# State-space decays from one single-pass product per head over all tokens, and outputs scaled as their roots arrive

## The chip, the cores and the metric

The kernel runs on one core of a Trainium2 chip. The metric is the device time of one execution in microseconds (us), the median of several runs. PE is the matrix engine (TensorE), PEld its weight loads, DVE is VectorE, ACT is ScalarE, POOL is GpSimd, SP is SyncE, which issues the weight DMAs.

## The reference

Two transformer blocks run over 256 tokens of width 1024. The change is in the first mixer of the second block, a state space layer of 16 heads of 64 values in two groups, whose result is independent of how the tokens are cut into chunks:

```
cs = cumsum(a)                       # a = dt * A, one number per token and head
L[l, s] = exp(cs[l] - cs[s]) for l >= s, else 0
y = (C B^T * L) @ X + D_skip * x_heads     # X = x_heads * dt; C, B shared by the 8 heads of a group
y = rmsnorm(y * silu(z)) per group of 512
```

The kernel takes chunks of 128 tokens, so there are two chunks (t = 0, 1), and the second also gets what the first leaves as state.

## The kernel before

The weights come through SP in tiles of 128x1024. Every product with them is made in three single-pass matmuls (fp32r type): ACT rounds a tile to its high part (line 954), DVE subtracts to get the low part (line 1405, `rest_of_tile`), and PE multiplies high by high, high by low and low by high (lines 357 to 359 for outputs with features on the partitions, 387 to 389 with tokens on the partitions). There are five slots for parts, so tile i can be rounded once PE has released tile i-5, and four slots for raw tiles. Small products are made in full fp32 with `group` (line 340); the profile shows one such matmul as two instructions.

All queues are written out by hand in program order. On PE, `step(n)` takes n pieces of the projections that lie ready as a filler (`fill`: z, gq, gk, gv, r, sig2, in this order): one piece of gq, gk or sig2 is 24 matmuls of 256 columns, one piece of z, gv or r is 12 of 512 columns. Four pieces make the two halves of gq: pieces 1 and 2 release the first two tiles, pieces 3 and 4 the next two. On ACT and DVE, `until(v)` first does all tile work, and all evacuations that were put behind (`put_behind`), whose release on PE comes before point v in PE's order; `full(name)` is `until` of that group and then a wait for it. `out_of(name)` waits until a PSUM bank was read, `settle` until the engine's own earlier results have landed.

The state space layer in the kernel before, in order on PE: 16 transposes of the convolved x (`xs`), the small product `dec`, one filler piece (gq 2), the C B^T products `CB` of both groups, and then the decays. There are eight (t, q) with four heads each (q = 0 to 3). For each, DVE multiplies the mask `after` by `a` (`seg_in`, 128x512), PE multiplies this in full fp32 with `upper` (`seg`: four matmuls of 128 columns), which gives cs[l] - cs[s] on the lower triangle, ACT takes Exp out of PSUM (line 1275), DVE multiplies by masked CB into `E`, and PE multiplies E by X (`diag`: four matmuls of 64 columns). After every second diag DVE adds it to the skip product and multiplies by silu(z), ACT sums squares (line 1294), POOL takes the root, DVE scales, and PE transposes (`y_out`) for the later product, with `y_T` on DVE and a rounding on ACT (line 1280). After the last `y_out` come one filler piece, the products `la` of the gated linear attention, and eight filler pieces, while DVE and ACT work out its gates.

Of the kernel before, what the change touches and what calls it, by code (L numbers as in the profile page):

```python
# [9 lines left out]
F32 = mybir.dt.float32  # L10
# [5 lines left out]
P = 128  # L16
# [32 lines left out]
    "pad", "conv_in", "conv", "silu", "gated", "Aexp", "dt", "soft_e", "soft", "soft_exp", "a", "X", "Xd", "La", "E",  # L49
# [34 lines left out]
def chunks(v, n):  # L84
    return v.rearrange("p (c n) -> p c n", c=n)
# [14 lines left out]
def build(nc, a, out):  # L100
    with ExitStack() as ctx:
# [32 lines left out]
        def f32(at, n):  # L134
            return room[:, at:at + n]
# [87 lines left out]
        dt_, e_, s_, s2_, p_, aa = (small[:, 32 * i:32 * i + 32] for i in range(6))  # L223
        Aexp, e1, d0 = (small[:, 192 + 16 * i:208 + 16 * i] for i in range(3))
        dt3 = dt_.rearrange("p (t h) -> p t h", t=2)
        a3 = aa.rearrange("p (t h) -> p t h", t=2)
# [15 lines left out]
        rot = [chunks(f32(8192 + 512 * i, 512), 4) for i in range(6)]  # L242
        La, E = rot[0:3], rot[3:6]
        quads = [(t, q) for t in range(2) for q in range(4)]
# [38 lines left out]
        def tensor(e):  # L283
# [481 lines left out]
            group(psum[:, b, 0:16], [(upper, a3[:, 1, :])])  # L765
            ends(group(psum[:, b, 16:32], [(after, a3[:, 0, :])]), "dec", b)
# [14 lines left out]
            yb = None  # L781

            def diag(i):
                nonlocal yb
                t, q = quads[i]
                g = q // 2
                if q % 2 == 0:
                    yb = bank()
                need(s["E"], i + 1)
                need(s["X"], t + 1)  # L790
                for h in range(4):
                    o = 256 * (q % 2) + 64 * h
                    last = group(psum[:, yb, o:o + 64], [(E[i % 3][:, h, :], X[:, t, 256 * q + 64 * h:256 * q + 64 * h + 64])])
                if q % 2 == 0:
                    where["diag", i] = Group(None, done(last), None)
                    return
                ends(last, ("y", t, g), yb)
                where["diag", i] = where["y", t, g]
                if t:
                    b = bank()  # L800
                    need(s["Xd"], 1)
                    out_of(("CB", g))
                    ends(group(psum[:, b, :], [(CB[:, g, P:256], Xd[:, 512 * g:512 * g + 512])]), ("yx", g), b)

            def y_out(t, g):
                need(s["y_out"], 2 * t + g + 1)
# [130 lines left out]
        def scalar(e):  # L937
# [332 lines left out]
            def seg(i):  # L1270
                full(("seg", i))
                if i >= 3:
                    until(where["diag", i - 3].at)
                    e.wait_ge(s["pe"], where["diag", i - 3].at)
                emptied(e.activation(E[i % 3], chunks(psum[:, where["seg", i].bank, :], 4), ACT.Exp), ("seg", i))

            def y_out(t, g):
                full(("yT", t, g))
                e.wait_ge(s["yT_gain"], 2 * t + g + 1)
# [4 lines left out]
            seg(1)  # L1284
            for i in range(8):
                if i + 2 < 8:
                    seg(i + 2)
                t, g = i // 4, (i % 4) // 2
                if i % 2:
                    full(("y", t, g))  # L1290
                    if t:
                        full(("yx", g))
                    e.wait_ge(s["y_sum"], 2 * t + g + 1)
                    e.activation(junk[:, 512 * g:512 * g + 512], xs[:, t, 512 * g:512 * g + 512], ACT.Square,
                                 accum_out=yss[:, 2 * t + g:2 * t + g + 1]).then_inc(s["y_sq"], 1)
                if i in (2, 4, 6):
                    y_out(*((0, 0), (0, 1), (1, 0))[i // 2 - 1])
            y_out(1, 1)
# [91 lines left out]
        def vector(e):  # L1390
# [387 lines left out]
            conv(3)  # L1778
            until(where["cv", 3].at + 3)
# [26 lines left out]
            e.wait_ge(s["a"], 1)  # L1806

# [6 lines left out]
            def seg_in(i):  # L1814
                t, q = quads[i]
                if i >= 3:
                    until(where["seg", i - 3].at)
                    e.wait_ge(s["pe"], where["seg", i - 3].at)
# [3 lines left out]
            seg_in(0)  # L1822
            seg_in(1)
# [18 lines left out]
            seg_in(2)  # L1842

            def seg(i):
                t, q = quads[i]
                until(where["seg", i].at)
                out_of(("seg", i))
                tt(E[i % 3], E[i % 3], bc(CB[:, q // 2, 256 * t:256 * t + P], 1, [P, 4, P]), ALU.mult).then_inc(s["E"], 1)

            def diag(i):  # L1850
                t, g = i // 4, (i % 4) // 2
                if i % 2 == 0:
                    return
                c, j = slice(512 * g, 512 * g + 512), 2 * t + g
                y = xs[:, t, c]
                step(tt(by_head(y), by_head(y), bc(row("ssd_D_2")[:, 8 * g:8 * g + 8], 2, [P, 8, 64]), ALU.mult))
# [17 lines left out]
                e.wait_ge(s["y_rstd"], j + 1)  # L1874
                ts(y, y, yrs[:, j:j + 1], ALU.mult).then_inc(s["y_out"], 1)

            def y_T(t, g):
                name, n = ("yT", t, g), 2 * t + g + 1
# [10 lines left out]
            seg(1)  # L1889
            for i in range(8):  # L1890
                if i + 3 < 8:
                    seg_in(i + 3)
                if i + 2 < 8:
                    seg(i + 2)
                diag(i)
                if i in (2, 4, 6):
                    y_T(*((0, 0), (0, 1), (1, 0))[i // 2 - 1])
            y_T(1, 1)
# [335 lines left out]
```

## Time and profile before

| | |
|---|---|
| median of 3 runs | 983.16 us (983.12 to 984.9) |
| profiled execution, its own time | 984.08 us |
| its span, first to last instruction | 982.0 us |
| PE busy | 963.7 us, 98% |
| DVE busy | 631.8 us, 64% |
| ACT busy | 506.0 us, 52% |
| granted TensorE clock, mean | 0.999 |

The span is what the rows below are times in; 2.1 us of the execution lie around it. Matmuls overlap in the pipeline, so that the rate of PE is read from the distance between starts and not from the duration of one.

### The profile page before, as it was taken

What the parts mean: (1) busy time and instruction counts of PE and PEld (TensorE: products, weight loads), DVE (VectorE), ACT (ScalarE), POOL (GpSimd) and SP (SyncE); (2) the same over time, 40 slices, a digit from 0 to 9 for tenths busy, and PEclk for the clock granted to TensorE, in tenths of its full rate; (3) what the DMA queues carried; (4) which work ended last, traced back from release to release, by engine and by line L of the source; (5) the groups of instructions that cost most, each with busy time, mean ns of one, the idle gap of its engine ahead of it and who ended that gap; (6) DMA issues with size and microseconds to landing.
All of it is one profiled execution on the core that took longest, in us unless ns stands there. A gap on an engine that the chain in (4) does not pass through costs nothing.

```text
span 982.0 us, 15896 instructions
## 1 busy us (share of the span) xinstructions
PE 963.7 (98%) x6552; PEld 871.7 (89%) x6552; DVE 631.8 (64%) x822; ACT 506.0 (52%) x744; POOL 52.5 (5%) x88
## 2 busy tenths in 40 slices
PE   7999999999999999999999999999999999999996
PEld 5877889989998898998988899998998899999995
DVE  5757676677555555687867687775554466555554
ACT  5565645655444444556644575544455444444442
POOL 3000001002000000300000002100100020000000
PEclk9999999999999999999999999999999999999999
DMA  8974445555665656465554556554755446565651
GB/s 272 314 243 129 113 125 154 170 172 173 210 196 175 191 183 198 121 191 171 183 159 114 148 152 193 154 191 129 237 168 155 127 151 211 176 198 175 198 179 43
DMA packets 135079, 170.36 MB, mean 173 GB/s; under 512 B 7664, under 2 KB 99104, under 8 KB 135008
## 3 DMA queue, kind: packets, MB, share of 16 engines
q1 hardware_dynamic: 133472, 165.47, 54.5%
q10 hardware_dynamic: 992, 2.58, 0.8%
q0 software_dynamic: 544, 1.31, 0.5%
q8 instruction: 52, 0.85, 0.4%
q14 instruction: 19, 0.16, 0.1%
HBM read 168.28 MB, written 1.05 MB: 172 GB/s over the span
## 4 chain that ended last, share of the span: by engine, by line
PE 90%; DVE 5%; ACT 3%; issue 1%; DMA 1%; DVEq 0%; POOLq 0%; POOL 0%; SPq 0%; ACTq 0%
PE ps L357 14%; PE ps L358 13%; PE ps L359 13%; PE ps L387 7%; PE ps L389 7%; PE ps L388 7%; PE ps L695 5%; PE ps L694 5%; PE ps L696 5%; PE ps L340 5%; PE ps L436 3%; DVE parts L1405 2%; PE ps L467 1%; PE ps L469 1%; PE ps L468 1%
## 5 line engine op out<-in xcount | busy, mean ns | idle before, releaser
L1405 DVE TENSOR_TENSOR parts<-raws,parts 128x1024 fp32r<-128x1024 f32 (+1 forms) x308 | 367.7, 1211 | 231.2 <-ACT parts L954 230.4
L954 ACT ACTIVATE parts<-raws 128x1024 fp32r<-128x1024 f32 (+1 forms) x308 | 315.6, 1043 | 247.0 <-PE ps L359 135.5
L357 PE MATMUL ps<-room_r,parts 128*128 128x256 f32 x1248 | 352.4, 282 | 0.9 <-DVE parts L1405 0.9
L358 PE MATMUL ps<-room_r,parts 128*128 128x256 f32 x1248 | 348.6, 279 | 0.0
L359 PE MATMUL ps<-room_r,parts 128*128 128x256 f32 x1248 | 348.5, 279 | 0.0
L357 PEld LDWEIGHTS ps<-room_r,parts 128*128 128x128 f32 x1248 | 234.7, 188 | 7.1 <-issue 3.9
L358 PEld LDWEIGHTS ps<-room_r,parts 128*128 128x128 f32 x1248 | 234.6, 188 | 1.3
L359 PEld LDWEIGHTS ps<-room_r,parts 128*128 128x128 f32 x1248 | 234.6, 188 | 0.0
L387 PE MATMUL ps<-parts,room_r 128*128 128x512 f32 (+1 forms) x336 | 136.2, 405 | 2.6 <-DVE parts L1405 2.6
L389 PE MATMUL ps<-parts,room_r 128*128 128x512 f32 (+1 forms) x336 | 132.0, 393 | 0.0
L388 PE MATMUL ps<-parts,room_r 128*128 128x512 f32 (+1 forms) x336 | 131.9, 393 | 0.0
L694 PE MATMUL ps<-parts,room_r 128*128 128x512 f32 x216 | 85.5, 396 | 0.0
L696 PE MATMUL ps<-parts,room_r 128*128 128x512 f32 x216 | 85.4, 396 | 0.0
L695 PE MATMUL ps<-parts,room_r 128*128 128x512 f32 x216 | 85.4, 396 | 0.0
L387 PEld LDWEIGHTS ps<-parts,room_r 128*128 128x128 f32 x336 | 63.9, 190 | 17.7 <-DVE parts L1405 3.2
L389 PEld LDWEIGHTS ps<-parts,room_r 128*128 128x128 f32 x336 | 63.7, 190 | 14.7
L388 PEld LDWEIGHTS ps<-parts,room_r 128*128 128x128 f32 x336 | 64.0, 190 | 13.4 <-issue 0.5
L1439 DVE TENSOR_TENSOR room_r<-room,room_r 128x512 fp32r<-128x512 f32 x43 | 29.8, 693 | 32.5 <-ACT room_r L1209 11.9
L696 PEld LDWEIGHTS ps<-parts,room_r 128*128 128x128 f32 x216 | 40.6, 188 | 9.7
L694 PEld LDWEIGHTS ps<-parts,room_r 128*128 128x128 f32 x216 | 40.6, 188 | 8.8
L695 PEld LDWEIGHTS ps<-parts,room_r 128*128 128x128 f32 x216 | 40.6, 188 | 8.7
L340 PE MATMUL ps<-room 128*128 128x256 f32 (+6 forms) x276 | 43.1, 311 | 0.4 <-ACT room L1089 0.4
(190 smaller groups left out, 838.8 us busy)
## 6 DMA issues: line engine op xcount, KB each, us to landing
raws<-in_w_in SPq DMA_DIRECT2D x100, 512.0 KB, 4.1
raws<-in_w_ffn_in SPq DMA_DIRECT2D x44, 512.0 KB, 4.6
raws<-in_w_up SPq DMA_DIRECT2D x32, 512.0 KB, 4.5
raws<-in_w_down SPq DMA_DIRECT2D x32, 512.0 KB, 4.4
raws<-in_w_ffn_out SPq DMA_DIRECT2D x22, 512.0 KB, 4.3
raws<-in_w_xkv SPq DMA_DIRECT2D x16, 512.0 KB, 4.4
raws<-in_w_out SPq DMA_DIRECT2D x8, 512.0 KB, 4.2
raws<-in_w_up_ssd SPq DMA_DIRECT2D x8, 512.0 KB, 4.7
```

The source lines that it names most:

```text
L340: last = e.matmul(ps, l, r, start=i == 0, stop=i == len(pairs) - 1)
L357: e.matmul(ps, wh, hT[0][:, k, :], start=k == 0, stop=False)
L358: e.matmul(ps, wh, hT[1][:, k, :], start=False, stop=False)
L359: last = e.matmul(ps, wl, hT[0][:, k, :], start=False, stop=k == K - 1)
L387: e.matmul(ps, hT[0][:, k, tok], wh, start=k == 0, stop=False)
L388: e.matmul(ps, hT[0][:, k, tok], wl, start=False, stop=False)
L389: last = e.matmul(ps, hT[1][:, k, tok], wh, start=False, stop=k == K - 1)
L694: e.matmul(ps, uh[:, k, tok], wh, start=q == 0 and k == 0, stop=False)
L695: e.matmul(ps, uh[:, k, tok], wl, start=False, stop=False)
L696: last = e.matmul(ps, ul[:, k, tok], wh, start=False, stop=q == n - 1 and k == 1)
L954: e.activation(t.h, t.raw, ACT.Copy).then_inc(s["hi"], 1)
L1405: e.tensor_tensor(t.l, t.raw, t.h.bitcast(F32), ALU.subtract).then_inc(s["lo"], 1)
```

## The change

The cumulative sums are made once for all heads. `a` for both chunks stands twice in a zeroed 128x256 array (`twice`, columns 0 to 15 and 32 to 47 of each chunk); two fp32 matmuls of 128 columns with `upper` give a bank `cs` with the sums of head n in row n and again in row 32+n, 256 tokens wide. ACT copies the bank as rounded fp32r (the high part), and DVE overwrites rows 32 to 47 with the remainder (the low part). For each head one fp32r matmul of 256 columns, with a 0/1 column `sel` (high row plus low row) broadcast over 128 columns as weights, spreads cs over all partitions for both chunks. ACT then makes relu(cs[s] - cs[l]) out of PSUM, 128 columns at a time with the per-partition sum as bias, and Exp with scale -1 for four heads at once from SBUF. Relu makes the part above the diagonal harmless, and CB stays masked. The order is now by q, with both chunks of a q in one round; the squares, roots and scales of an output are split off into `y_squares`, `y_part` and `y_scaled`. `y_out` of group 0 is issued before the diags of q = 2, that of chunk 0, group 1 one piece after the last diag, and the last `y_out` two pieces after that. The number of filler pieces from `dec` to `la` is 24 before and after, of which two now lie between the last `y_out` and `la`. On DVE CB's evacuation comes before the product `Xd`, and the low part of cs between them.

```diff
+        twice = f32(8192, 256).rearrange("p (t c) -> p t c", t=2)
+        a3 = twice[:, :, 0:16]
+        cs, sel = room_r[:, 8448:8704], room_r[:, 8704:8720]
+        decays = [chunks(f32(9216 + 512 * i, 512), 4) for i in range(4)]
+        E = lambda t, q: decays[2 * (q % 2) + t]
...
# PE
-            group(psum[:, b, 0:16], [(upper, a3[:, 1, :])])
-            ends(group(psum[:, b, 16:32], [(after, a3[:, 0, :])]), "dec", b)
+            group(psum[:, b, 0:32], [(upper, a3)])
+            ends(group(psum[:, b, 32:48], [(after, a3[:, 0, :])]), "dec", b)
...
-            def seg(i):
-                b = bank()
-                need(s["La"], i + 1)
-                for h in range(4):
-                    last = group(psum[:, b, h * P:h * P + P], [(La[i % 3][:, h, :], upper)])
-                ends(last, ("seg", i), b)
+            def seg(q):
+                out_of("cs")
+                need(s["sel"], 1)
+                for i in range(2):
+                    b = bank()
+                    for h in range(2):
+                        n = 4 * q + 2 * i + h
+                        last = group(psum[:, b, 256 * h:256 * h + 256], [(sel[:, n:n + 1].to_broadcast([P, P]), cs)])
+                    ends(last, ("seg", q, i), b)
...
-            seg(0)
-            seg(1)
-            step(5)
-            for i in range(8):
-                if i + 2 < 8:
-                    seg(i + 2)
-                step()
-                diag(i)
-                if i < 6:
-                    step()
-                if i in (2, 4, 6):
-                    y_out(*((0, 0), (0, 1), (1, 0))[i // 2 - 1])
-            step(3)
+            b = bank()
+            need(s["a_twice"], 1)
+            for t in range(2):
+                last = group(psum[:, b, t * P:t * P + P], [(twice[:, t, :], upper)])
+            ends(last, "cs", b)
+            step()
+            seg(0)
+            step(3)
+            for q in range(4):
+                if q < 3:
+                    seg(q + 1)
+                step()
+                if q == 2:
+                    y_out(0, 0)
+                diag(0, q)
+                step()
+                if q == 2:
+                    y_out(1, 0)
+                diag(1, q)
+                step(2 if q < 3 else 1)
+            y_out(0, 1)
+            step(2)
             y_out(1, 1)
-            step()
+            step(2)
...
# ACT
-            step(e.activation(e1, psum[:, where["dec"].bank, 0:16], ACT.Exp))
-            emptied(e.activation(d0, psum[:, where["dec"].bank, 16:32], ACT.Exp), "dec")
+            step(e.activation(sums_, psum[:, where["dec"].bank, 0:32], ACT.Copy))
+            full("cs")
+            e.activation(cs, psum[:, where["cs"].bank, 0:256], ACT.Copy).then_inc(s["cs_hi"], 1)
+            step(e.activation(e1, psum[:, where["dec"].bank, 16:32], ACT.Exp))
+            emptied(e.activation(d0, psum[:, where["dec"].bank, 32:48], ACT.Exp), "dec")
+            settle()
...
-                emptied(e.activation(E[i % 3], chunks(psum[:, where["seg", i].bank, :], 4), ACT.Exp), ("seg", i))
+                for i in range(2):
+                    full(("seg", q, i))
+                    v = psum[:, where["seg", q, i].bank, :].rearrange("p (h t n) -> p h t n", h=2, t=2)
+                    for t in range(2):
+                        for h in range(2):
+                            n = 4 * q + 2 * i + h
+                            inst = e.activation(E(t, q)[:, 2 * i + h, :], v[:, h, t, :], ACT.Relu,
+                                                bias=sums3[:, t, n:n + 1], scale=-1.0)
...
+                settle()
+                for t in range(2):
+                    out_of(("seg", q, 1))
+                    e.activation(E(t, q), E(t, q), ACT.Exp, scale=-1.0).then_inc(s["decays"], 1)
...
# DVE, behind conv(3) and behind conv(5)
+            step(e.memset(twice, 0.0))
+            tt(sel, ident[:, 0:16], ident[:, 32:48], ALU.add).then_inc(s["sel"], 1)
...
+            e.tensor_copy(twice[:, :, 32:48], a3).then_inc(s["a_twice"], 1)
...
-                tt(La[i % 3], bc(after, 1, [P, 4, P]), bc(a3[:, t, 4 * q:4 * q + 4], 2, [P, 4, P]),
-                   ALU.mult).then_inc(s["La"], 1)
...
-            until(where["dec"].at)
-            out_of("dec")
-            e.wait_ge(s["X"], 1)
-            tt(by_head(Xd), by_head(X[:, 0, :]), bc(d0, 2, [P, 16, 64]), ALU.mult).then_inc(s["Xd"], 1)
             for g in range(2):
                 name = ("CB", g)
                 full(name)
...
                 emptied(e.tensor_copy(CB[:, g, P:256], v[:, P:256]), name)
+            until(where["cs"].at)
+            rows_ = slice(32, 48)
+            e.wait_ge(s["cs_hi"], 1)
+            emptied(tt(cs[rows_, :], bank_of("cs")[rows_, 0:256], cs[rows_, :].bitcast(F32), ALU.subtract), "cs")
+            until(where["dec"].at)
+            out_of("dec")
+            e.wait_ge(s["X"], 1)
+            tt(by_head(Xd), by_head(X[:, 0, :]), bc(d0, 2, [P, 16, 64]), ALU.mult).then_inc(s["Xd"], 1)
...
+            def y_scaled(t, g):
+                y, n = xs[:, t, 512 * g:512 * g + 512], 2 * g + t
+                until(where["y", t, g].at + 1)
+                e.wait_ge(s["y_rstd"], n + 1)
+                ts(y, y, yrs[:, n:n + 1], ALU.mult).then_inc(s["y_out"], 1)
...
+            for q in range(4):
+                if q < 3:
+                    seg(q + 1)
+                for t in range(2):
+                    if q % 2:
+                        y_part(t, q // 2)
+                        y_scaled(t, q // 2)
+                    else:
+                        y_skip(t, q // 2)
+                if q == 2:
+                    for t in range(2):
+                        y_T(t, 0)
+            for t in range(2):
+                y_T(t, 1)
```

## Rows read from the trace of the kernel before

**Rows 1.** The page: busy time of the engines.

```profile
PE 963.7 (98%) x6552; PEld 871.7 (89%) x6552; DVE 631.8 (64%) x822; ACT 506.0 (52%) x744; POOL 52.5 (5%) x88
```

**Rows 2.** The waits of PE from 440 to 700 us: us in total, times, longest.

```profile
PE ps L357 <- DVE parts L1405: 0.9, 3, 0.4
```

**Rows 3.** The timeline of PE, the last of CB and seg(0), seg(1): start, duration.

```profile
472.27 1.95 PE L340 MATMUL ps<-consts,room 128*128 128x128 f32 x16
473.98 0.36 PE L357 MATMUL ps<-room_r,parts 128*128 128x256 f32 x1
474.18 0.28 PE L358 MATMUL ps<-room_r,parts 128*128 128x256 f32 x1
474.30 0.28 PE L359 MATMUL ps<-room_r,parts 128*128 128x256 f32 x1
```

**Rows 4.** The timeline of PE, a later seg (2) and what follows it.

```profile
488.06 1.05 PE L340 MATMUL ps<-consts,room 128*128 128x128 f32 x8
488.87 0.36 PE L357 MATMUL ps<-room_r,parts 128*128 128x256 f32 x1
```

**Rows 5.** The timeline of DVE from the products X to seg_in(2).

```profile
472.78 3.60 DVE L1439 TENSOR_TENSOR room<-room 128x1024 f32<-128x1024 f32 x3
476.30 1.22 DVE L1405 TENSOR_TENSOR parts<-raws,parts 128x1024 fp32r<-128x1024 f32 x1
477.44 0.68 DVE L1439 TENSOR_TENSOR room<-ps,rows_rstd 128x512 f32<-128x512 f32 x1
478.04 1.22 DVE L1405 TENSOR_TENSOR parts<-raws,parts 128x1024 fp32r<-128x1024 f32 x1
...
480.36 0.68 DVE L1439 TENSOR_TENSOR room<-consts,room 128x512 f32<-128x512 f32 x1
```

**Rows 6.** Groups by line and shape, whole span: busy us, mean ns of one, idle before.

```profile
L1182 ACT ACTIVATE junk<-ps 128x128 f32<-128x128 f32 x8 | 2.1, 289 | 0.7 <-PE ps L340 0.7
...
L1439 DVE TENSOR_TENSOR room<-ps,consts 128x256 f32<-128x256 f32 x4 | 1.7, 417 | 0.0
```

**Rows 7.** The timeline of ACT: the copies xs, and two tiles.

```profile
471.50 2.06 ACT L988 ACTIVATE room<-ps 128x512 f32<-128x512 f32 x4
...
475.01 2.01 ACT L954 ACTIVATE parts<-raws 128x1024 fp32r<-128x1024 f32 x2
```

**Rows 8.** The timeline of PE: a start after a wait for a tile.

```profile
460.25 0.50 PE L387 MATMUL ps<-parts,room_r 128*128 128x512 f32 x1 [0.69 <-DVE parts L1405]
460.59 0.40 PE L388 MATMUL ps<-parts,room_r 128*128 128x512 f32 x1
460.82 0.40 PE L389 MATMUL ps<-parts,room_r 128*128 128x512 f32 x1
```

**Rows 9.** The timeline of DVE, sum and scale of one output.

```profile
517.67 0.68 DVE L1439 TENSOR_TENSOR room<-ps,room 128x512 f32<-128x512 f32 x1
...
520.85 0.49 DVE L1442 TENSOR_SCALAR room<-room,ssq 128x512 f32<-128x512 f32 x1 [1.77 <-POOL ssq L2042]
```

**Rows 10.** The timeline of DVE behind conv(3): the tile after the next one.

```profile
447.63 1.23 DVE L1405 TENSOR_TENSOR parts<-raws,parts 128x1024 fp32r<-128x1024 f32 x1 [0.87 <-ACT parts L954]
```

**Rows 11.** The timeline of PE, behind la.

```profile
577.55 0.28 PE L359 MATMUL ps<-room_r,parts 128*128 128x256 f32 x1
578.09 0.38 PE L357 MATMUL ps<-room_r,parts 128*128 128x256 f32 x1 [0.26 <-DVE parts L1405]
```

**Rows 12.** The timeline of DVE, the bias of la.

```profile
556.27 1.66 DVE L1442 TENSOR_SCALAR room<-ps,cols 128x256 f32<-128x256 f32 x4
```

**Rows 13.** The timeline of PE at the start: two of its first 512-column matmuls.

```profile
11.14 0.80 PE L387 MATMUL ps<-parts,room_r 128*128 128x512 f32 x1 [1.94 <-DVE parts L1405]
...
16.83 0.40 PE L388 MATMUL ps<-parts,room_r 128*128 128x512 f32 x1
```

**Rows 14.** Windows behind the last matmul: PE, PEld, DVE, ACT, POOL busy, clock, DMA.

```profile
974.00:976.00 2.00, 0.35 (x2) 0.00 (x0) 0.94 (x3) 1.27 (x4) 0.55 (x1) 1.00 0.00 0
...
979.00:980.00 1.00, 0.00 (x0) 0.00 (x0) 0.55 (x1) 0.00 (x0) 0.00 (x0) 0.67 0.23 90
```

More of the change, by code:

```diff
@@ L47 @@
     "ret_sq", "ret_rstd", "ret", "oT_hi", "retT_hi", "gates", "mix", "mix_hi", "mixT", "up", "up_hi", "upT",
-    "pad", "conv_in", "conv", "silu", "gated", "Aexp", "dt", "soft_e", "soft", "soft_exp", "a", "X", "Xd", "La", "E",
+    "pad", "conv_in", "conv", "silu", "gated", "Aexp", "dt", "soft_e", "soft", "soft_exp", "a", "a_twice", "sel", "cs_hi", "decays", "X", "Xd", "E",
     "y_sq", "y_sum", "y_rstd", "y_out", "yT_gain", "yT_hi", "yT", "la", "la_min", "la_ln", "bcum", "bexp", "qt", "kt",
@@ L222, in build @@
         small = r2.take(256)
-        dt_, e_, s_, s2_, p_, aa = (small[:, 32 * i:32 * i + 32] for i in range(6))
+        dt_, e_, s_, s2_, p_, sums_ = (small[:, 32 * i:32 * i + 32] for i in range(6))
         Aexp, e1, d0 = (small[:, 192 + 16 * i:208 + 16 * i] for i in range(3))
         dt3 = dt_.rearrange("p (t h) -> p t h", t=2)
-        a3 = aa.rearrange("p (t h) -> p t h", t=2)
+        twice = f32(8192, 256).rearrange("p (t c) -> p t c", t=2)
+        a3 = twice[:, :, 0:16]
+        sums3 = sums_.rearrange("p (t h) -> p t h", t=2)
+        cs, sel = room_r[:, 8448:8704], room_r[:, 8704:8720]
         at_zs = r2.at
@@ L772, in tensor, with diag @@
                 ends(group(psum[:, b, 256:384], [(cv[:, 8 + g, P:256], cv[:, 10 + g, P:256])]), ("CB", g), b)
-            def seg(i):
-                b = bank()
-                need(s["La"], i + 1)
-                for h in range(4):
-                    last = group(psum[:, b, h * P:h * P + P], [(La[i % 3][:, h, :], upper)])
-                ends(last, ("seg", i), b)
[L781 to L785, printed above, removed]
+            def seg(q):
[7 more added lines that the diff above has]
+                    ends(last, ("seg", q, i), b)
+            yb = [None, None]
+            def diag(t, q):
                 g = q // 2
                 if q % 2 == 0:
-                    yb = bank()
-                need(s["E"], i + 1)
+                    yb[t] = bank()
+                need(s["E"], 2 * q + t + 1)
                 need(s["X"], t + 1)
@@ L792, in diag @@
                     o = 256 * (q % 2) + 64 * h
-                    last = group(psum[:, yb, o:o + 64], [(E[i % 3][:, h, :], X[:, t, 256 * q + 64 * h:256 * q + 64 * h + 64])])
+                    last = group(psum[:, yb[t], o:o + 64],
+                                 [(E(t, q)[:, h, :], X[:, t, 256 * q + 64 * h:256 * q + 64 * h + 64])])
                 if q % 2 == 0:
-                    where["diag", i] = Group(None, done(last), None)
+                    where["diag", t, q] = Group(None, done(last), None)
                     return
-                ends(last, ("y", t, g), yb)
-                where["diag", i] = where["y", t, g]
+                ends(last, ("y", t, g), yb[t])
+                where["diag", t, q] = where["y", t, g]
                 if t:
@@ L1266, in scalar @@
             full("dec")
-            step(e.activation(e1, psum[:, where["dec"].bank, 0:16], ACT.Exp))
-            emptied(e.activation(d0, psum[:, where["dec"].bank, 16:32], ACT.Exp), "dec")
[L1270 to L1274, printed above, removed]
-                emptied(e.activation(E[i % 3], chunks(psum[:, where["seg", i].bank, :], 4), ACT.Exp), ("seg", i))
+            step(e.activation(sums_, psum[:, where["dec"].bank, 0:32], ACT.Copy))
@@ new lines, in scalar, with seg @@
+            full("cs")
[3 more added lines that the diff above has]
+            settle()
+            def seg(q):
+                if q >= 2:
+                    until(where["diag", 1, q - 2].at)
+                    e.wait_ge(s["pe"], where["diag", 1, q - 2].at)
+                for i in range(2):
[6 more added lines that the diff above has]
+                                                bias=sums3[:, t, n:n + 1], scale=-1.0)
+                            if t and h:
+                                emptied(inst, ("seg", q, i))
+                            else:
+                                step(inst)
+                settle()
+                for t in range(2):
+                    out_of(("seg", q, 1))
+                    e.activation(E(t, q), E(t, q), ACT.Exp, scale=-1.0).then_inc(s["decays"], 1)
@@ L1277, in y_out, with y_squares @@
+            def y_squares(t, g):
+                n = 2 * g + t
+                full(("y", t, g))
+                if t:
+                    full(("yx", g))
+                e.wait_ge(s["y_sum"], n + 1)
+                e.activation(junk[:, 512 * (n % 2):512 * (n % 2) + 512], xs[:, t, 512 * g:512 * g + 512], ACT.Square,
+                             accum_out=yss[:, n:n + 1]).then_inc(s["y_sq"], 1)
             def y_out(t, g):
                 full(("yT", t, g))
-                e.wait_ge(s["yT_gain"], 2 * t + g + 1)
+                e.wait_ge(s["yT_gain"], 2 * g + t + 1)
@@ L1283, in scalar @@
             seg(0)
[L1284 to L1298, printed above, removed]
+            for q in range(4):
[3 more added lines that the diff above has]
+                    for t in range(2):
+                        y_squares(t, q // 2)
+                if q == 2:
+                    for t in range(2):
+                        y_out(t, 0)
+            for t in range(2):
+                y_out(t, 1)
             full(("la", 1))
@@ L1812, in vector @@
             put_behind(projections2())
[L1814 to L1818, printed above, removed]
-                tt(La[i % 3], bc(after, 1, [P, 4, P]), bc(a3[:, t, 4 * q:4 * q + 4], 2, [P, 4, P]),
-                   ALU.mult).then_inc(s["La"], 1)
-            seg_in(0)
-            seg_in(1)
             by_head = lambda v: v.rearrange("p (h d) -> p h d", d=64)
@@ L1840, in vector, with seg, y_skip, y_part @@
                 emptied(e.tensor_copy(CB[:, g, P:256], v[:, P:256]), name)
-            settle()
[L1842 to L1854, printed above, removed]
+            until(where["cs"].at)
[6 more added lines that the diff above has]
+            tt(by_head(Xd), by_head(X[:, 0, :]), bc(d0, 2, [P, 16, 64]), ALU.mult).then_inc(s["Xd"], 1)
+            settle()
+            def seg(q):
+                for t in range(2):
+                    until(where["seg", q, 1].at)
+                    e.wait_ge(s["decays"], 2 * q + t + 1)
+                    v = E(t, q)
+                    tt(v, v, bc(CB[:, q // 2, 256 * t:256 * t + P], 1, [P, 4, P]), ALU.mult).then_inc(s["E"], 1)
+            def y_skip(t, g):
+                y = xs[:, t, 512 * g:512 * g + 512]
+                step(tt(by_head(y), by_head(y), bc(row("ssd_D_2")[:, 8 * g:8 * g + 8], 2, [P, 8, 64]), ALU.mult))
+            def y_part(t, g):
+                c = slice(512 * g, 512 * g + 512)
                 y = xs[:, t, c]
-                step(tt(by_head(y), by_head(y), bc(row("ssd_D_2")[:, 8 * g:8 * g + 8], 2, [P, 8, 64]), ALU.mult))
                 full(("y", t, g))
@@ L1873, in diag @@
                 tt(y, y, zs[:, t, c], ALU.mult).then_inc(s["y_sum"], 1)
-                e.wait_ge(s["y_rstd"], j + 1)
-                ts(y, y, yrs[:, j:j + 1], ALU.mult).then_inc(s["y_out"], 1)
+            def y_scaled(t, g):
[3 more added lines that the diff above has]
+                ts(y, y, yrs[:, n:n + 1], ALU.mult).then_inc(s["y_out"], 1)
             def y_T(t, g):
-                name, n = ("yT", t, g), 2 * t + g + 1
+                name, n = ("yT", t, g), 2 * g + t + 1
                 full(name)
@@ L1888, in vector @@
             seg(0)
[L1889 to L1898, printed above, removed]
+            for q in range(4):
+                if q < 3:
+                    seg(q + 1)
+                for t in range(2):
+                    if q % 2:
+                        y_part(t, q // 2)
+                        y_scaled(t, q // 2)
+                    else:
+                        y_skip(t, q // 2)
+                if q == 2:
+                    for t in range(2):
+                        y_T(t, 0)
+            for t in range(2):
+                y_T(t, 1)
             e.wait_ge(s["yT"], 4)
```

5 lines of the change are left out of this document (1 added, 4 removed).

## The prediction

> **What bounds the kernel now.** I read the page first, then PE's waits, then the timelines of PE, DVE and ACT around the decays. PE is busy 98% of the span and DVE 64% [rows 1], so PE's queue sets the end: work taken out of it is gained, and a wait put into it is lost, one for one. From 440 to 700 us PE waits for small products at no place; on filler pieces of the 256-column kind it loses 0.9 us in three waits for a tile's low part [rows 2]. Between 463 and 556 us, where the decays lie, its timeline has no gap. So the cuts on ACT and DVE are worth nothing by themselves there, and the question is what the change takes from PE, and whether the new chain cs, ACT, DVE, seg arrives in time.
>
> **PE's work.** Seg(0) and seg(1) are 16 rows of 128 columns in full fp32 and take 473.98 - 472.27 = 1.71 us, 0.107 each [rows 3]. A filler matmul of 256 columns starts 0.12 us behind the one before (474.18 to 474.30; 0.117 over a piece), but the first after fp32 work takes 0.20, so a switch costs 0.09 [rows 3]. A later seg takes 488.87 - 488.06 = 0.81 [rows 4], with its switch 0.90; there are six. Removed: 1.71 + 6 x 0.90 = 7.11 us.
>
> Added are the two fp32 matmuls for cs, four rows of 0.107, 0.43 us, and 16 fp32r matmuls of 256 columns. None like these, with one column broadcast as weights, stands in the trace. From below the filler's 0.117 each, 1.87 us; from above the fp32 rate, four rows of 0.107 for 256 columns, 6.8 us in all. I take 1.87, because type, width and weights of 128 columns are the filler's. They need no switch. Counting the places where fp32 work goes over to fp32r, there are 18 between `dec` and `la` before, six of them the late segs', and 13 after: one more, 0.09. `dec` has 32 columns instead of 16, still four rows near the floor: nothing. Sum on PE: -7.11 + 0.43 + 1.87 + 0.09 = -4.7 us.
>
> The Trainium skill (FP8 and Floating Point Precision, TensorE Precision Notes) says that true fp32 takes four passes through the array and the reduced form reads fp32 and truncates. By it a head's 256 columns would fall from four passes to one, and the sum would stay the one above.
>
> **The new wait.** Seg(0) stands one filler piece behind cs and needs the low rows from DVE. PE finishes CB at 472.27 as before [rows 3]; cs to 472.70, the piece (gq 3) with switch 2.90 more: PE stands at seg(0) at 475.6.
>
> DVE is late. In its order the low part of cs comes after X(0), X(1), after all that `until(CB)` pulls in, and after the six CB operations. The row of three 1024-column products holds X(0), X(1) and Xd, and the tile behind starts at 476.30, so one costs 1.17 [rows 5]. X(0) can't start before 472.78, since it waits behind a tile's low part and for ACT's copies xs, which begin at 471.50 [rows 7]. Then, by distances of starts [rows 5]: two X 2.35, tile 1.14, gq's evacuation 0.60, tile and CB together 478.04 to 480.36 = 2.32. So CB ends at 472.78 + 6.41 = 479.19. Moving Xd behind has been counted: it is the 1.17 that is gone. The low part is 256 columns out of PSUM, as the row of 0.417 us [rows 6]: 479.61, and PE gets the semaphore some 0.07 later, 479.68. PE then restarts; after a wait the first distance is 0.34 [rows 8] where 0.23 is normal, 0.11 lost. The stall: 479.68 - 475.60 + 0.11 = 4.2 us. The two operations of `seg_in` that DVE loses before X free nothing, since after them it waited for ACT's rounding anyway.
>
> ACT's part is not the last: it copies xs until 473.6, then `full(cs)` makes it round two tiles, 0.95 to 1.0 each [rows 7], then copies cs, under 0.6: ready at 476.2 at the latest, three us before DVE asks. Exp's table load comes behind it.
>
> Bounds of the stall. From below: if the two tiles and gq's evacuation (1.14 twice and 0.60, 2.9) came after the low part, 1.3 us. But where `until` puts them is fixed by their releases, all before CB on PE. From above: another tile's 1.2 in front, 5.4.
>
> **What else is behind it.** After the stall DVE makes Xd, until 480.8, then waits for seg(0)'s decays. ACT pays eight Relu of 128 columns each, between 0.13 (a quarter of a 512-column copy's 0.515 [rows 7]) and 0.29 [rows 6], then two Exp of 512, 0.55 each. I take 0.2, since short instructions carry a fixed part. From PE's first bank at 480.1 the Relus end by 482.5 even at the upper price, Exp by 483.7, DVE's products until 484.4, then the tile that was let go at 481.6, low part ready by 486. PE wants it for gk 3, three pieces and seg(1) after 480.2, at 489.1. Three us of slack, and the decays of q are wanted a whole round (some 14 us) after their seg. The 32 Relu cost ACT some 6 us, 9 at most, hidden by its 48% of idle time [rows 1]; with that cover gone they would come at 2 us per q on PE.
>
> Outputs: from the sum to the scale's end one takes 521.34 - 517.67 = 3.7 us [rows 9], the second chunk's two 512-column operations more, 5.1. A piece of 12 x 0.233 with its switch is 2.9 [rows 3, 8]. y(0,1) is wanted after two pieces and a diag of 0.8 or more, over 6 us. y(1,1) stands behind it on DVE, ready 8.8 us after y(0,1) was made; a tile between makes it 11.2 at most, and it is wanted after four pieces, a diag and four transposes, some 13. No wait, by 2 us. `memset` and `sel` come in front of a tile behind which DVE idles 0.87 for ACT [rows 10]; at 0.42 [rows 6] and at most that again for 16 columns they fit, just. With no such idle they would be up to 0.8 of stall.
>
> **Behind la.** At 578.09 PE loses 0.43 before and 0.10 at the restart, for a tile that DVE reaches late [rows 11]. DVE has been in one chain since la's bias, which begins at 556.27 because `y_T(1,1)` is in the way [rows 12], though PE had the first bank at some 555.6. The last y_T is now one piece earlier, so the chain starts as PE delivers, 0.5 earlier at its end: I take 0.4 of the 0.53 as gained; bounds 0 and 0.53.
>
> **Sum:** -4.7 + 4.2 - 0.4 = -0.9 us. Against the profiled execution, 984.1, that is 983.2; this execution was 0.9 above the median of 983.16, so the median becomes 982.3.
>
> **The rivals.** Less than 0.2% (2.0 us) is no difference that can be told on this kernel.
>
> *No real stall (faster).* The low part comes before the tiles, or PE's waits cost less: at 1.3 us the sum is -3.8, 979.4. To pass 0.2% the stall has to stay under 3.1. For it: cover of 4 us could be had by a few other orders of DVE's queue. Against it: each operation in front is a row. Chance 0.16.
>
> *The clock falls in the stall (slower).* At the start 13 matmuls of 512 columns took 16.83 - 11.14 = 5.69 us, where at full rate they take 13 x 0.233 = 3.03 [rows 8, 13]: TensorE was at 1.2 GHz and lost 2.7 us. After the last matmul, about 974.4, the granted clock fell at some 979.3, 5 us on [rows 14]. A stall of 4.2 us is near that. If the clock falls, PE resumes at half rate; with the start's 2.7 us, -0.9 + 2.7 = +1.8, 984.9, and from 2.9 us of loss it is measurably slower. One fall after 5 us idle speaks against it at 4.2. The Trainium skill (TensorE: Matmul & The Clock Gate, Part 1) has it that the throttled state is the default and activity releases it, which is this rival's mechanism; it would give 984.9 here. Chance 0.14.
>
> *The waits are longer, or another one comes up (slower).* Relus at the upper price, a tile late at gk 3, or the stall of 5.4: from +0.3 to +3, 984.5. Chance 0.08.
>
> *The product isn't single-pass:* 4.9 us more on PE, 987.3. Chance 0.02.
>
> **Numbers.** The forecast has 0.60; its own range is 981.3 to 983.5, from the bounds of la's wait, 0.5 on the stall and 0.3 on the matmuls. The range from 980.6 to 985.0 leaves out most of the fast rival and the tail of the slow ones. Faster than 981.2: 0.18. Within: 0.70. Slower than 985.1: 0.12.
>
> **What would show it.** PE's wait before the first seg for a DVE product into room_r, about 4 us, near 475.6 to 479.7; 16 matmuls of 256 columns at 0.117 with 4 fp32 rows for cs, and the 64 rows of the old seg gone. ACT: 32 Relu of 128 columns without table loads between. The granted clock at 1.0 behind the stall. No wait at gk 3 nor at a y_out, and none at la's eighth piece. The prediction is wrong if the wait is far from 4 us, if the clock dips, or if a broadcast column loads slower than 0.117.

## The result and the profile after

| | before | after |
|---|---|---|
| median of 5 runs | 983.12 us (982.71 to 984.9) | 987.38 us (986.26 to 988.24) |
| ratio | | 1.0042, 95% interval 1.0031 to 1.0052 |
| profiled execution: span | 982.0 us | 986.4 us |
| mean granted clock | 0.999 (profiled); 0.996 to 0.999 in the later runs | 0.993 to 0.995 (all five) |

The kernel became slower by 0.4%, against a forecast of 982.3 us. The page of the kernel after, busy time and clock by slices:

```profile
PE 961.6 (97%) x6508; PEld 869.1 (88%) x6508; DVE 628.2 (64%) x818; ACT 514.0 (52%) x778; POOL 53.3 (5%) x88
...
PEclk9999999999999999999899999999999999999999
```

PE has 44 instructions fewer, as the count of the change says (64 gone, 20 come), ACT 34 more. The dip of the clock is in the slice that begins at 468 us. In it, on the timeline of PE (start, duration):

```profile
480.09 1.22 PE L345 MATMUL ps<-room_r 128*128 128x256 f32 x4 [3.99 <-DVE room_r L1479]
481.11 0.41 PE L362 MATMUL ps<-room_r,parts 128*128 128x256 f32 x1
481.32 0.41 PE L363 MATMUL ps<-room_r,parts 128*128 128x256 f32 x1
...
484.73 0.35 PE L364 MATMUL ps<-room_r,parts 128*128 128x256 f32 x1
484.93 0.28 PE L362 MATMUL ps<-room_r,parts 128*128 128x256 f32 x1
485.04 0.28 PE L363 MATMUL ps<-room_r,parts 128*128 128x256 f32 x1
```

The first row is seg(0), after an idle 3.99 us for the low rows of cs. Behind it the filler matmuls start 0.21 us apart instead of the 0.117 of full rate, until 484.9. The windows of the same kernel (length; PE, PEld, DVE, ACT, POOL busy; clock; DMA) tell why:

```profile
478.00:479.00 1.00, 0.00 (x0) 0.00 (x0) 1.00 (x5) 0.00 (x0) 0.00 (x0) 0.53 0.78 221
479.00:480.00 1.00, 0.00 (x0) 0.00 (x0) 0.97 (x4) 0.00 (x0) 0.00 (x0) 0.50 0.94 307
480.00:484.00 4.00, 3.91 (x18) 3.92 (x19) 1.28 (x3) 2.93 (x10) 0.00 (x0) 0.50 0.40 126
484.00:485.00 1.00, 1.00 (x7) 1.00 (x6) 1.00 (x2) 1.00 (x2) 0.00 (x0) 0.56 0.00 0
485.00:486.00 1.00, 1.00 (x11) 1.00 (x10) 0.89 (x2) 0.46 (x2) 0.00 (x0) 1.00 0.00 0
```

The granted clock falls at 478.1, two us after PE's last matmul has ended, and is back at 484.9: TensorE runs at 1.2 GHz for 4.8 us of work. On DVE the low part comes as counted [rows 5]; the timeline of DVE after:

```profile
473.17 2.36 DVE L1479 TENSOR_TENSOR room<-room 128x1024 f32<-128x1024 f32 x2
475.44 1.22 DVE L1445 TENSOR_TENSOR parts<-raws,parts 128x1024 fp32r<-128x1024 f32 x1
476.58 0.68 DVE L1479 TENSOR_TENSOR room<-ps,rows_rstd 128x512 f32<-128x512 f32 x1
477.18 1.22 DVE L1445 TENSOR_TENSOR parts<-raws,parts 128x1024 fp32r<-128x1024 f32 x1
...
479.61 0.42 DVE L1479 TENSOR_TENSOR room_r<-ps,room_r 16x256 fp32r<-16x256 f32 x1
```

The second loss is behind la. Where PE lost 0.53 us at one place by the distance of its starts [rows 11], it now waits at two; timeline of PE:

```profile
556.50 1.99 PE L345 MATMUL ps<-room,wa 16*128 16x256 f32 x8
...
578.75 0.35 PE L362 MATMUL ps<-room_r,parts 128*128 128x256 f32 x1 [0.43 <-DVE parts L1445]
...
582.20 0.38 PE L362 MATMUL ps<-room_r,parts 128*128 128x256 f32 x1 [1.81 <-DVE parts L1445]
```

The bias, which began 1.8 us behind PE's first la product (556.27 [rows 12]; PE had started la at 554.45), begins 3.9 us behind it. Timeline of DVE:

```profile
553.36 2.36 DVE L1445 TENSOR_TENSOR parts<-raws,parts 128x1024 fp32r<-128x1024 f32 x2 [0.25 <-ACT parts L971]
555.63 0.69 DVE L1479 TENSOR_TENSOR room<-ps,cols 128x512 f32<-128x512 f32 x1
557.08 0.69 DVE L1479 TENSOR_TENSOR room_r<-room,room_r 128x512 fp32r<-128x512 f32 x1 [0.76 <-ACT room_r L1324]
559.25 1.22 DVE L1445 TENSOR_TENSOR parts<-raws,parts 128x1024 fp32r<-128x1024 f32 x1 [1.49 <-ACT parts L971]
560.40 1.65 DVE L1482 TENSOR_SCALAR room<-ps,cols 128x256 f32<-128x256 f32 x4
```

Between the last `y_T` and the bias stands a tile, and DVE idles 1.49 us for ACT's rounding of it. Before, none stood there.

The account by distances of starts on PE: from `dec` to la 86.7 us before (467.71 to 554.45), 88.4 after (468.10 to 556.50), +1.7; from la to the first product of the gated attention 25.2 before, 27.3 after (583.79), +2.05; the start of the kernel +0.4 (PE waits 5.7 us for the first input instead of 5.3), the rest +0.3. Together 4.4, the difference of the spans. Executions of one kernel differ by some 3 us (the one before: 981.2 to 984.3 in the later runs), so the runs below are compared by medians, by ratios to the kernel before, and by inner stretches. A difference of medians and one of ratios can be 1 us apart.

### The profile page after: what moved, and what is told of

It reads as the page before. It is cut to its first block, busy times and chain, and to the rows that moved or that the text cites. A ratio compares the mean times of both kernels' runs of the same rounds, so it can differ in the third digit from the quotient of the medians.

```text
span 986.4 us, 15833 instructions
## 1 busy us (share of the span) xinstructions
PE 961.6 (97%) x6508; PEld 869.1 (88%) x6508; DVE 628.2 (64%) x818; ACT 514.0 (52%) x778; POOL 53.3 (5%) x88
## 4 chain that ended last, share of the span: by engine, by line
PE 89%; DVE 6%; ACT 3%; issue 1%; DMA 1%; DVEq 0%; POOLq 0%; POOL 0%; SPq 0%; ACTq 0%
PE ps L362 14%; PE ps L364 13%; PE ps L363 13%; PE ps L392 7%; PE ps L394 7%; PE ps L393 7%; PE ps L701 5%; PE ps L700 5%; PE ps L699 5%; PE ps L345 4%; PE ps L441 3%; DVE parts L1445 2%; DVE room L1479 1%; DVE room L1485 1%; PE ps L472 1%; PE ps L473 1%
```

## The experiments

All ran in turn with the kernel before, whose median was 983.04 us in the first group of runs, 982.87 in the second and 982.82 in the third. The table names the group.

| | group | median us | ratio to before, 95% interval |
|---|---|---|---|
| seg(0) two pieces later | 1 | 982.14 | 0.9986 to 1.0004 |
| last output one piece later | 1 | 985.40 | 1.0016 to 1.0036 |
| both | 1 | 979.85 | 0.9964 to 0.9983 |
| PE kept busy in the wait | 1 | 984.59 | 1.0013 to 1.0034 |
| la's bias before the tile | 2 | 983.94 | 1.0006 to 1.0025 |
| both, and last output behind la's bias | 2 | 982.16 | 0.9979 to 0.9997 |
| low rows first | 2 | 981.38 | 0.9981 to 0.9998 |
| both, every Relu twice | 2 | 988.95 | 1.0050 to 1.0073 |
| two waits gone | 3 | 978.41 | 0.9942 to 0.9968 |
| two waits gone, product in full fp32 | 3 | 983.32 | 0.9999 to 1.0016 |
| DVE's order alone | 3 | 978.77 | 0.9944 to 0.9971 |

**Seg(0) two pieces later.**

```diff
-            step()
+            step(3)
             seg(0)
-            step(3)
+            step()
```

> The changed kernel with seg(0) three filler pieces behind cs instead of one, and one piece behind it instead of three. Theory A (PE waits 4.0 us for DVE's low rows of cs, and the clock falls to 1.2 GHz in that wait and costs 2.25 us more; behind la another 2.05 us are lost for a reason of its own): PE arrives at seg(0) some 1.5 us after the low rows are there, no wait, granted clock at 1.0 throughout, 987.4 - 4.1 - 2.25 = 981.0 us; the wait behind la stays at 2.5 us. Rival B (the 2.25 us belong to the new single-pass product with its broadcast weights and not to the clock): 983.3, with slow matmuls behind seg(0) still. Rival C (the wait behind la is a consequence of the first one): 979.

982.14 us, 5.2 less than the kernel after (4.6 by the ratios) and 1.1 more than theory A said. There is no wait at seg(0), its four matmuls take 0.47, and the clock is up there, so rival B is out. The timeline of PE:

```profile
481.07 0.63 PE L345 MATMUL ps<-room_r 128*128 128x256 f32 x4
481.54 0.28 PE L362 MATMUL ps<-room_r,parts 128*128 128x256 f32 x1
```

The waits behind la stay, against C. In this execution the clock fell behind la instead; windows:

```profile
576.00:577.00 1.00, 1.00 (x9) 1.00 (x7) 0.00 (x0) 0.99 (x2) 0.00 (x0) 0.77 0.49 86
577.00:579.00 2.00, 2.00 (x26) 1.78 (x25) 0.17 (x1) 2.00 (x4) 0.00 (x0) 0.50 0.66 224
```

PE lost 0.6 and 2.0 us there in two waits for a tile, with 12 filler matmuls between them. It was back at work from 575.3, and the clock fell at 576.5. From la to the second product of the gated attention PE takes 32.9 us, 1.5 more than in the kernel after. That is a price of the waits behind la that theory A left out.

**Last output one piece later**, and both edits.

```diff
             y_out(0, 1)
-            step(2)
+            step(3)
             y_out(1, 1)
-            step(2)
+            step()
```

> The changed kernel with the last y_out three pieces behind y_out(0, 1) and one piece before la, instead of two and two. Theory A (with two pieces before la DVE finds one more tile between y_T(1, 1) and la's bias, and ACT is late with its high part): DVE's bias starts within 2 us of PE's first la matmul instead of 3.9, the waits behind la fall from 2.5 to about 0.5 us, 985.4 us. Rival C (the late bias comes from the first wait, or from the two y_T that now stand together): 987.4, no change.

> Both edits. Theory A, where the parts add: 981.0 - 2.0 = 979.0 us, the 4.7 us of PE's work nearly whole against 983.1 before. Rival D (something else behind takes the place of a wait that goes, since DVE and ACT have the same work in less time): 980.5 or more.

The first gave the 985.4 that theory A named, but its trace doesn't show what it said: the stretch from la to the gated attention fell from 27.3 to 26.65 us only, with one wait of 1.67 us left. The other part isn't in this trace; six of nine executions had a mean clock of 0.997 where the kernel after has 0.995 at most, which points to shorter falls. Inconclusive by itself. Both together gave 979.85, between theory A's 979.0 and the 980.5 of rival D. The bias started 3.2 us behind la in both kernels, where 2 had been expected: the tile went from behind the last `y_T` to before it.

**PE kept busy in the wait.** It computes nothing that is used.

```diff
+                first = bank()
+                if q == 0:
+                    for _ in range(18):
+                        group(psum[:, first, 0:P], [(twice[:, 0, :], upper)])
                 out_of("cs")
...
-                    b = bank()
+                    b = bank() if i else first
```

> The changed kernel with 18 full-fp32 matmuls of 128 columns of no use, 18 x 0.213 = 3.8 us, on PE in front of seg(0)'s wait, into a bank that seg(0) overwrites. Theory A (it is the idle time that lets the clock fall): PE resumes at the same moment, the granted clock stays at 1.0, 987.4 - 2.25 = 985.1 us. Rival B (the product's own slowness): 987.4, and seg(0)'s four matmuls still take 1.0 us.

The timeline of PE:

```profile
474.22 4.18 PE L345 MATMUL ps<-consts,room 128*128 128x128 f32 x36
478.38 0.74 PE L345 MATMUL ps<-room_r 128*128 128x256 f32 x4
478.95 0.28 PE L362 MATMUL ps<-room_r,parts 128*128 128x256 f32 x1
479.07 0.28 PE L363 MATMUL ps<-room_r,parts 128*128 128x256 f32 x1
```

The 36 rows fill 4.2 us, seg(0) takes 0.57 and the filler goes on at 0.12. The time is 984.59: 2.8 us by the medians, 1.9 by the ratios, came back for work of no use in a wait of the same length. The clock stayed up in the profiled execution: it was the idle time that let it fall.

**Low rows first** moves the subtraction into cs from behind the loop over CB to in front of it, without the tile work that `until` would do.

```diff
+            rows_ = slice(32, 48)
+            e.wait_ge(s["cs_hi"], 1)
+            emptied(tt(cs[rows_, :], bank_of("cs")[rows_, 0:256], cs[rows_, :].bitcast(F32), ALU.subtract), "cs")
             for g in range(2):
                 name = ("CB", g)
```

> The changed kernel, where DVE makes the low rows of cs right behind the two X, in front of the two tiles, the evacuation and CB. Theory A (what stands in front on DVE makes the wait of seg(0), and its length lets the clock fall): DVE waits for ACT's high rows until 476.2, the wait on PE falls from 4.0 to about 1.0 us, the clock stays up, 987.4 - 3.0 - 2.25 = 982.1. Rival (the clock falls by a shorter wait as well): 984.4. The waits behind la stay.

```profile
473.77 0.74 PE L345 MATMUL ps<-room_r 128*128 128x256 f32 x4 [0.58 <-DVE room_r L1479]
```

PE, in its timeline above, waits 0.58 us instead of 3.99 and the clock stays up: 981.38, 0.7 below theory A's 982.1 and far from the rival's 984.4.

**La's bias before the tile.**

```diff
             for i in range(2):
                 name = ("la", i)
-                full(name)
+                e.wait_ge(s["pe"], where[name].at)
```

> The changed kernel, where DVE waits for the la products without doing tile work first, so that the tile that stood behind the last y_T (at 559.25, after an idle 1.49 us for ACT) comes behind la's bias. Theory A (this tile is what delays the gates' chain): the bias starts some 2.4 us sooner, the waits behind la fall from 2.5 us to 0.5 or less, 985.2 us in the scale where the changed kernel has 987.4 and the one before 983.1. Rival C (the chain is late because both outputs of group 1 stand in front of it, and a tile less gives only a part): 986.5 or more.

The timeline of DVE, where PE began la at 554.32:

```profile
554.92 0.69 DVE L1479 TENSOR_TENSOR room_r<-room,room_r 128x512 fp32r<-128x512 f32 x1 [0.76 <-ACT room_r L1324]
555.65 1.66 DVE L1482 TENSOR_SCALAR room<-ps,cols 128x256 f32<-128x256 f32 x4
```

The bias starts 1.3 us behind la, one wait of 0.21 us is left behind it, and the stretch from la on falls to 25.0. The median fell to 983.94, 3.4 below the kernel after (2.7 by the ratios) where 2.2 were expected. The tile in front was the cause; two outputs in front of the bias (rival C) don't hurt by themselves.

A part of the surplus is in the clock. The wait at seg(0) is the same, but here the clock fell later and was back sooner. The timeline of PE and the windows:

```profile
478.54 0.93 PE L345 MATMUL ps<-room_r 128*128 128x256 f32 x4 [3.99 <-DVE room_r L1479]
```

```profile
478.00:479.00 1.00, 0.46 (x3) 0.46 (x4) 0.94 (x3) 0.00 (x0) 0.00 (x0) 0.96 0.84 139
...
482.00:483.00 1.00, 1.00 (x10) 1.00 (x9) 0.86 (x2) 1.00 (x3) 0.00 (x0) 0.84 0.00 0
```

It fell at 478.9, 4.4 us after the last matmul and with PE already back at work, and rose at 482.3. From seg(0) to seg(1) PE took 10.5 us, where it takes 11.1 in the kernel after and 9.0 with the clock up (PE kept busy, or the low rows first). So one and the same wait cost 2.2 us of clock in one execution and 1.5 in another.

**Last output behind la's bias**, on top of both edits. On DVE `y_T(1, 1)` goes behind `la_min`, and with it the wait for all outputs and the line that puts the evacuations of the second gates behind; on ACT `y_out(1, 1)` goes behind Exp and Ln.

```diff
# ACT
             e.activation(tmpg, tmpg, ACT.Ln, bias=1.0).then_inc(s["la_ln"], 1)
+            y_out(1, 1)
# DVE
             stt(tmpg, la, -1.0, la, ALU.mult, ALU.min).then_inc(s["la_min"], 1)
+            y_T(1, 1)
```

> The kernel with both edits (seg(0) two pieces later, last y_out one piece later), where besides DVE and ACT do the last output's y_T behind la's bias, in the time in which they waited for each other for Exp and Ln. Theory C (the wait of 1.95 us behind la is left because DVE has two outputs' work in front of la's bias instead of one): the bias starts within 1.4 us of PE's first la product instead of 3.2, the wait behind la goes, 979.85 - 1.9 = 978.0. Rival (the chain's own length, not its start, sets the wait, now that y_T(1, 1) is in it): 979.5 to 980.

A miss: 982.16, slower than without it by 2.3 (1.4 by the ratios). The bias did start 1.2 us behind la, but the next step, which needs Ln, came 9.4 us behind the bias instead of 6.5. The timeline of ACT and the row of DVE that waits:

```profile
554.58 1.28 ACT L1344 ACT_TABLE_LOAD   x1
555.87 1.06 ACT L1344 ACTIVATE big<-big 128x1024 f32<-128x1024 f32 x1
556.84 0.61 ACT L1324 ACTIVATE room_r<-room 128x512 fp32r<-128x512 f32 x1
```

```profile
557.48 0.69 DVE L1479 TENSOR_TENSOR room_r<-room,room_r 128x512 fp32r<-128x512 f32 x1 [3.78 <-ACT room_r L1324]
```

DVE's `y_T` now waits for a rounding that stands behind Exp, a table load and Ln on ACT. The waits on PE behind la were back at 0.43 and 1.81 us, and in this execution too the clock fell behind them. From la to the second product of the gated attention PE takes 33.0 us instead of 30.8 with both edits alone. The kernel after, with the same two waits and the clock up, takes 31.4, so that 0.6 us of the loss are waits and 1.6 the clock. Four of the twelve executions took 979.2 to 981.1 us, the other eight 982.1 to 982.5.

**Every Relu twice**, on top of both edits; the same result.

```diff
+                            step(e.activation(E(t, q)[:, 2 * i + h, :], v[:, h, t, :], ACT.Relu,
+                                              bias=sums3[:, t, n:n + 1], scale=-1.0))
+                            settle()
                             inst = e.activation(E(t, q)[:, 2 * i + h, :], v[:, h, t, :], ACT.Relu,
```

> The kernel with both edits with every one of the 32 Relu done twice, the second after the first has landed; it computes the same. Theory A (ACT's part of the decays is hidden): some 2.9 us more of ACT in each of four rounds and no difference, 979.85, +-0.3. Rival (ACT is the late one in the rounds, and the 32 Relu of the change cost time on the path): up to 2.9 us a round, 982 or more.

988.95, 9 us more: a miss for theory A. A round's Relu took 5.3 us instead of 2.2. PE waits now, in the round of q = 3; timelines of PE in this kernel and of ACT in the kernel with both edits:

```profile
524.56 0.77 PE L392 MATMUL ps<-parts,room_r 128*128 128x512 f32 x1 [3.53 <-issue]
```

```profile
512.97 2.15 ACT L1301 ACTIVATE room<-ps,room 128x128 f32<-128x128 f32 x8
515.22 1.16 ACT L1310 ACTIVATE room<-room 128x512 f32<-128x512 f32 x2
```

PE starts as the last Relu (524.09) has ended, and by the order in which banks go round, the filler piece behind diag(1, 2) takes the bank that seg(3) filled. With single Relus ACT had emptied it by 515.1, and PE wanted it at 518.2: 3.1 us of slack. The doubling alone takes that in one round, and a round's delay goes on into the next: counted from `dec`, the Exp of q = 2 comes 4.4 us later here and the last Relu of q = 3 7.6 us later. So the 32 Relu of the change were hidden, as the trace of the kernel after shows too (no wait in the rounds), but by 3 us and not by a whole round. The clock fell twice in the middle of this execution, in this wait and behind la, and the 9 us hold that too.

**Two waits gone**: seg(0) two pieces later and la's bias before the tile, and the same with the product in full fp32, and with DVE's two edits alone.

```diff
-[(sel[:, n:n + 1].to_broadcast([P, P]), cs)]
+[(sel[:, n:n + 1].bitcast(F32).to_broadcast([P, P]), cs.bitcast(F32))]   # product in full fp32
```

> The changed kernel with seg(0) three pieces behind cs and with la's bias in front of the tile, each of which took its wait away in a run of its own. If both causes are right and independent: no wait at seg(0), 0.5 us or less behind la, granted clock at 1.0 from start to end, and what is left is PE's saved work, 4.7 us: 983.1 - 4.7 = 978.4, +-0.7. If something else takes their place: 980 or more.

> The same kernel with the 16 products sel x cs in full fp32 instead of fp32r, the values as before. By rows of the old kernel each is 0.427 us instead of 0.117, and four of the segs now need a switch back of 0.09: 16 x 0.31 + 0.36 = 5.3 us more than the kernel with two waits gone, about 983.7, so that the single pass would be worth all of the change's gain. If the product is not one pass, or the broadcast weights are what it costs: no more than 2 us.

> The changed kernel with PE's order left alone and two edits on DVE: the low rows of cs right behind X, and la's bias in front of the tile. Wait of 0.9 at seg(0) as in the run with the low rows first, 0.5 behind la, no fall of the clock: 0.9 us above the kernel with two waits gone, 979.3. If the short wait counts for more than its length (clock): 981 or more.

All three within 0.6 us of what was expected: 978.41, 983.32, 978.77. The waits of PE from start to end in the first (total, times, longest):

```profile
PE ps L441 <- DMA x<-in_x: 5.6, 2, 5.2
PE ps L392 <- DVE parts L1445: 2.6, 2, 1.9
PE ps L441 <- ACT big L1168: 1.4, 1, 1.4
PE ps L362 <- DVE parts L1445: 0.9, 3, 0.4
PE ps L345 <- ACT room L1106: 0.4, 1, 0.4
```

These are the waits that the kernel before has: 5.3, 2.6, 1.4, 0.9 [rows 2] and 0.4 us. From `dec` (468.18) to la (550.14) PE takes 81.96 us, 4.78 less than before. With the product in full fp32 the stretch has 5.1 more. The two kernels' rows for it, of the first and then of the one in full fp32 (durations in ns):

```profile
L345 PE MATMUL ps<-room_r x16: 276/279/282, 481.6 to 513.0; 128*128 128x256 f32 x16
```

```profile
L345 PE MATMUL ps<-room_r x32: 377/379/379, 480.2 to 516.5; 128*128 128x256 f32 x32
```

Four products take 0.47 us by their starts as single pass and 1.54 in full fp32; the timeline of PE in the latter:

```profile
480.17 1.89 PE L345 MATMUL ps<-room_r 128*128 128x256 f32 x8
481.71 0.47 PE L362 MATMUL ps<-room_r,parts 128*128 128x256 f32 x1
```

The version with two waits gone is 0.45% faster than the kernel before (ratio 0.9955) and 0.9% faster than the change as it was made.

## Why the prediction was wrong

**What bounds the kernel: right.** PE's queue sets the end; each wait that came or went by a microsecond or more showed in the time.

**PE's work: right.** -4.7 forecast, -4.78 measured with the waits gone. The single pass with a broadcast column costs the filler's 0.117, as taken.

**The new wait: right in place, cause and size.** 475.6 to 479.7 forecast, 475.9 to 480.1 measured. The low rows first and seg(0) later each took it away.

**The clock: the step that failed first.** The sum put it at nothing, and it was a rival with a chance of 0.14. It happened in the profiled execution, and the mean clock of all five (0.993 to 0.995, where the kernel before has 0.996 at least) points to it in each. The trace had one fall, 5 us after the last matmul [rows 14], and I read "5 us" as if less were safe. One fall tells when the clock was down, not how little idle time is enough: here it fell 2 us after PE stopped, and 4.4 us after in the run with la's bias in front of the tile. By the spacings, seg(0) took 1.02 instead of 0.47 and the three pieces behind it 10.1 instead of 8.4, together 2.25 us; the runs with PE kept busy and with the wait gone gave it back. The rival's price, 2.7, was about right; its sum, 984.9, fell short mainly by the next point. I took that price from the start of the kernel, where the matmuls start 0.43 us apart instead of 0.233. The granted clock of the same profile reads 1.00 there:

```profile
12.00:13.00 1.00, 1.00 (x3) 0.73 (x3) 1.00 (x2) 0.95 (x2) 0.00 (x0) 1.00 0.64 113
```

With the last output behind la's bias the clock of that stretch reads 0.50 from 12 to 15 us, with the starts 0.43 us apart there too. So a profile can lack the slow start, and mean clocks can differ by 0.002 for that reason alone.

**Behind la: the second step that failed, and with its sign.** I took 0.4 us as gained because the last `y_T` is one piece earlier. It is, but what I compared was the place of `y_out` with la, and not what `until` puts between them on DVE: with two pieces there instead of one another tile is released before la, `full` does it first, and ACT has it late. Measured +2.05 us on PE; with the bias in front of that tile it was gone. If something is moved past work that has no fixed place in a queue, such as tiles, that work has to be laid out anew, as I had done for seg(0). -0.4 was forecast, so this term is 2.4 off, the clock 2.25: together 4.7 of the miss of 5.1 us. The slow range ended at 985.0 because the clock was considered alone and the loss behind la not at all. The chances were also cut at 981.2 and 985.1 and not at the ends of the range, 980.6 and 985.0.

**ACT hidden: right for the change, for a reason of which I had not seen all.** I gave the decays a whole round of slack; the bank gives 3.1 us. A Relu of 128 columns costs 0.27 by its starts, not the 0.2 that I took, inside the bounds.

**Outputs, `memset` and `sel`: right**, no wait came of them. What stays open is how much of the gain of 2 us with the last output one piece later was clock and how much was waiting, and why the clock falls sooner or later after the same wait, and behind la in some executions and not in others.

## What to carry to other kernels

When PE's queue is the bound, a chain of small steps over ACT and DVE that a matmul waits for has to be laid out with all the work that those queues do first, tiles and evacuations too. Here two filler pieces, or one subtraction moved forward, were worth some 5 us (4.6 and 5.1 by the ratios), as much as the arithmetic saved. A wait of 4 us on PE had a second price here, the clock, of 1.5 to 2.2 us. Such a price has to be put into the sum and not into the tail. If a piece of filler is moved, look for which tile it releases, and in front of whose critical step that tile lands.

## What the runs showed of the hardware

TensorE's granted clock fell to 1.2 GHz 2.0 us after its last matmul in the kernel after, 4.4 us after it in the run with la's bias in front of the tile (the same wait of 3.99 us; PE was back at work), and 5 us after it at the end of the kernel before [rows 14]. It came back 4.8 us after work had resumed in the first and 3.8 us after in the second. The wait cost 6.4 us in all in the kernel after (4.15 by the starts, and 2.25 of clock). Behind la it fell in some executions after PE had lost 0.6 and 2.0 us, with 12 filler matmuls between the two waits and more behind them: no single wait there was longer than 1.8 us. A stationary operand that is one column read 128 times cost nothing extra: the matmuls start 0.117 us apart as with a full one. Of a full-fp32 product of 256 columns each of its two instructions took 0.19 us by the starts (1.54 for eight), less than twice the 0.107 of 128 columns.
